# Norms ahead of the feed-forward stages in two halves of the tokens, and four PSUM banks at the merge

## What is computed

```python
# block a
mixed = sigmoid(ga) * ya + sigmoid(gb) * yb           # yb = r @ w_b
x = x + mixed @ w_out
h2 = x * rsqrt(mean(x * x) + EPS) * g_mlp              # over the features
x = x + square(relu(h2 @ w_up)) @ w_down
# block b
merged = sigmoid(gate_a) * ya + sigmoid(gate_b) * yb
x = layer_norm(DN_ALPHA * x + merged @ w_out + b_out, ln1_g, ln1_b)
x = layer_norm(DN_ALPHA * x + conv_ffn(x), ln2_g, ln2_b)
```

## Time and profile before

| | |
|---|---|
| median of three runs | 3595.11 us |
| the profiled execution | 3596.14 us |
| its span, first to last instruction | 3594.4 us |
| mean granted clock of TensorE | 0.985 |
| busy: PE, DVE, ACT, POOL | 3444.3, 1591.8, 1432.2, 1445.8 us |

### The profile page before, as it was taken

The page is one execution under the profiler, slowest core; times in us unless marked ns, Lnnn a source line. Parts: engine busy times, 40 slices in busy tenths (PEclk is TensorE's granted clock), DMA queues, the critical chain, the costliest instruction groups (busy, mean ns, idle before and its releaser), DMA issues.

```text
span 3594.4 us, 45460 instructions
## 1 busy us (share of the span) xinstructions
PE 3444.3 (96%) x16338; PEld 2792.4 (78%) x16338; DVE 1591.8 (44%) x2423; ACT 1432.2 (40%) x2114; POOL 1445.8 (40%) x1100
## 2 busy tenths in 40 slices
PE   7999999999999999999999999999999999999997
PEld 6788778887688778887768876787777688767785
DVE  5724232226623332227861444434478514344435
ACT  4735233224734332224462444333344534353333
POOL 3334444444334444444323342444343233434442
PEclk9999999999999999999999999999999999999999
DMA  3121222222112222222212121222212121222221
GB/s 142 59 83 71 94 93 95 93 95 94 69 72 91 91 88 94 94 105 73 83 36 83 68 88 71 94 93 93 82 72 71 54 75 61 95 69 94 93 93 59
DMA packets 43812, 298.49 MB, mean 83 GB/s; under 512 B 4816, under 2 KB 5456, under 8 KB 8592
## 3 DMA queue, kind: packets, MB, share of 16 engines
q1 hardware_dynamic: 41696, 291.52, 22.7%
q10 hardware_dynamic: 1968, 4.94, 0.4%
HBM read 294.34 MB, written 2.10 MB: 82 GB/s over the span
## 4 chain that ended last, share of the span: by engine, by line
issue 54%; POOL 32%; PE 11%; DVE 1%; ACT 1%; POOLq 1%; DVEq 0%; ACTq 0%
POOL w_lo L310 32%; PE ps L432 4%; PE ps L434 3%; PE ps L433 3%; PE ps L516 0%; POOLq L305 0%; DVE arena L1640 0%; ACT arena L1115 0%; POOLq L309 0%; DVE x L1675 0%; DVE arena L1663 0%; DVE tmp L1470 0%; ACT y_hi L1134 0%; DVE x L1912 0%; ACT x L1433 0%
## 5 line engine op out<-in xcount | busy, mean ns | idle before, releaser
L310 POOL TENSOR_TENSOR w_lo<-w_raw,w_hi 128x512 fp32r<-128x512 f32 x1096 | 1445.6, 1351 | 2106.1 <-ACT w_hi L936 2106.1
L432 PE MATMUL ps<-x_hi,w_hi 128*128 128x512 f32 x2752 | 1098.9, 399 | 23.0 <-DVE x_lo L1455 18.4
L433 PE MATMUL ps<-x_lo,w_hi 128*128 128x512 f32 x2752 | 1076.8, 391 | 0.0
L434 PE MATMUL ps<-x_hi,w_lo 128*128 128x512 f32 x2752 | 1076.7, 391 | 0.0
L936 ACT ACTIVATE w_hi<-w_raw 128x1024 fp32r<-128x1024 f32 x548 | 547.5, 1048 | 503.9 <-PE ps L434 503.9
L432 PEld LDWEIGHTS ps<-x_hi,w_hi 128*128 128x128 f32 x2752 | 519.9, 189 | 172.2 <-issue 38.1
L434 PEld LDWEIGHTS ps<-x_hi,w_lo 128*128 128x128 f32 x2752 | 519.7, 189 | 111.3
L433 PEld LDWEIGHTS ps<-x_lo,w_hi 128*128 128x128 f32 x2752 | 520.4, 189 | 106.0 <-issue 2.4
L432 PE MATMUL ps<-y_hi,w_hi 128*128 128x512 f32 x1248 | 490.9, 393 | 20.4 <-DVE x L1675 13.0
L433 PE MATMUL ps<-y_lo,w_hi 128*128 128x512 f32 x1248 | 487.1, 390 | 0.0
L434 PE MATMUL ps<-y_hi,w_lo 128*128 128x512 f32 x1248 | 486.7, 390 | 0.0
(11 more groups left out here) (184 smaller groups left out, 3139.0 us busy)
## 6 DMA issues: line engine op xcount, KB each, us to landing
w_raw<-stream SPq DMA_DIRECT2D x274, 1024.0 KB, 4.8
x<-x_t SPq DMA_DIRECT2D x4, 512.0 KB, 5.7
rotary<-rot ACTq DMA_DIRECT2D x4, 512.0 KB, 3.6
y_t<-x SPq DMA_DIRECT2D x8, 256.0 KB, 2.1
ct<-consts ACTq DMA_DIRECT2D x2, 770.0 KB, 4.7
arena<-pos ACTq DMA_DIRECT2D x2, 256.0 KB, 3.4
vec<-vectors ACTq DMA_DIRECT2D x4, 116.0 KB, 2.0
ct<-consts ACTq DMA_DIRECT2D x1, 128.0 KB, 4.1
```

Of the source, the lines that this page charges most:

```text
L310: ins = nc.gpsimd.tensor_tensor(WL[:, s, c:c + S], RAW[:, s, c:c + S], WH[:, s, c:c + S].bitcast(F32), ALU.subtract)
L432: pe.matmul(ps, wh, xh, start=(k == 0), stop=False)
L433: pe.matmul(ps, wh, xl, start=False, stop=False)
L434: return pe.matmul(ps, wl, xh, start=False, stop=last)
```

## The change

Three things are changed. First, in `mixer_gemms` of TensorE the ring of banks is 4 long from the last gates on. Second, wo panels 2 and 3 are worked by `gemm_halves`: all four tiles for tokens 0 to 255, then all four for tokens 256 to 511; the first two up panels are worked the same way (`first_up`). So a panel's slot is released only in the second half. Third, the norm ahead of the feed-forward stage (n2 in a, ln1 in b; twice each) is made for each half by itself: its small products stand in TensorE's order at the places given as `beside`, and the steps of DVE and ACT, each on 256 columns, are written out in an order that mixes both halves with the additions of wo and the casts of the panels. `keep_clock` is gone from these four norms. ACT's `hi` can now be issued in two parts (`hi_first`, `hi_part`). The norm ln2 of block b and the ones at the start of the layers stay. The four negated sinks are computed behind the norm of a layer instead of ahead of it.

The diff, cut to its core (the first part is TensorE's, then ACT's, then DVE's; blank lines are left out):

```diff
+            def gemm_halves(n, xh, xl, name, beside):
...
+                banks = [next_bank(name(j)) for j in range(4)]
+                for h in range(2):
+                    for j in range(4):
+                        s = (n + j // 2) % 2
+                        if h == 0 and j % 2 == 0:
+                            pe.wait_ge(lo_ready, n + j // 2 + 3)
+                        T.after(("read",) + name(j) + (0,) if h else bank_reader[banks[j]], own=False)
+                        for k in range(KD):
+                            c = (k * 2 + j % 2) * P
+                            mm = split_products(PS[:, banks[j], HS[h]], k, k == KD - 1, WH[:, s, c:c + P], WL[:, s, c:c + P],
+                                                xh[:, k, HS[h]], xl[:, k, HS[h]])
+                        T.done(mm, *name(j), h)
+                        if h:
+                            bank_reader[banks[j]] = ("read",) + name(j) + (1,)
+                            if j % 2:
+                                marks[("panel", n + j // 2)] = marks[name(j) + (1,)]
+                        if (h, j) in beside:
+                            beside[h, j]()
...
+            def mixer_gemms(l, w, t, gates, beside):
+                ring[0] = 4
                 for _ in gates:
...
-                for p in range(4):
+                for p in range(2):
                     (gemm if p else gemm_first)(w["wo"] + p, KD, 2, XH, XL, lambda k: (t, l, "merged_lo", k),
                          lambda m: (t, l, "wo", 2 * p + m))
-
-            def ffn(l, t, ff, groups, kt, base_t, base_d, base_h, h_ready):
+                gemm_halves(w["wo"] + 2, XH, XL, lambda j: (t, l, "wo", 4 + j), beside)
...
+            def ffn(l, t, ff, groups, kt, base_t, base_d, base_h, h_ready, beside):
...
-                for b in range(4):
-                    T.after(bank_reader[b], own=False)
+                def first_up():
+                    if l or t == "b":
+                        pe.wait_ge(up_read, base_t)
+                    for h in range(2):
+                        for p in range(2):
+                            if h == 0:
+                                pe.wait_ge(lo_ready, ff + p + 3)
+                                T.after(*bank_reader[2 * p:2 * p + 2], own=False)
+                            s = (ff + p) % 2
+                            for k in range(KD):
+                                if p == 0:
+                                    T.after(h_ready(k, h), own=False)
+                                for m in range(2):
+                                    c = (k * 2 + m) * P
+                                    mm = split_products(PS[:, 2 * p + m, HS[h]], k, k == KD - 1, WH[:, s, c:c + P],
+                                                        WL[:, s, c:c + P], XH[:, k, HS[h]], XL[:, k, HS[h]])
+                                    if h and k == KD - 1:
+                                        mm.then_inc(up_full, 1)
+                                if (h, p, k) in beside:
+                                    beside[h, p, k]()
...
-                        if isinstance(g, int) and g == 0 and p == 0:
...
+                mixer_gemms(l, w, t, gates, {(1, 0): lambda: deviation(0), (1, 1): lambda: spread_half(0)})
+                ffn(l, t, w["ff"], FF1_GROUPS, 4, *bases(t, l), lambda k, h: (t, l, "h2_lo", k, h),
+                    {(0, 0, 2): lambda: deviation(1), (0, 0, 6): lambda: spread_half(1)})
...
+                def mean(h):
...
+                    T.after((t, l, "ln1_sum", KD - 1, h), bank_reader[bank], own=False)
+                    T.done(pe.matmul(PS[:, bank, 0:HN], CT[:, 128:256], TMP[:, 2, HS[h]], start=True, stop=True),
+                           t, l, "ln1_mean", h)
...
+                def mean_square(h):
+                    bank = 5 + 2 * h
+                    T.after(bank_reader[bank], own=False)
+                    for k in range(KD):
+                        T.after((t, l, "ln1_sq", k, h), own=False)
+                        mm = pe.matmul(PS[:, bank, 0:HN], CT[:, 128:256], AR[:, 20 + k, HS[h]], start=(k == 0), stop=(k == KD - 1))
+                    T.done(mm, t, l, "ln1_ms", h)
...
+                mixer_gemms(l, w, t, gates, {(1, 0): lambda: mean(0), (1, 2): lambda: mean_square(0)})
+                ffn(l, t, w["ff"], FF2_GROUPS, 2, *bases(t, l), lambda k, h: (t, l, "ln1_lo", k, h),
+                    {(0, 0, 6): lambda: mean(1), (0, 1, 7): lambda: mean_square(1)})
...
+            def hi_first(c):
+                act.wait_ge(raw_full[c % 2], 16 * (c // 2 + 1))
+                who, n = marks.get(("panel", c - 2), ("pe", 1))
+                act.wait_ge(sems[who], n)
+                hi_part(c % 2, 0)
...
+                def square(k, *h):
+                    c = HS[h[0]] if h else slice(0, S)
+                    free = max(k - 2, 1)
+                    A.after(("read", t, l, "wo", k, *h), (t, l, "n2_acc", free, *(h if free >= 4 else ())) if k >= 2 else None)
+                    A.done(act.activation(TMP[:, k % 2, c], X[:, k, c], ACT.Square), t, l, "n2_sq", k, *h)
...
+                hi(w["wo"] + 2)
+                square(0)
+                square(1)
+                hi(w["wo"] + 3)
+                square(2)
+                square(3)
+                warm_root()
+                for k in range(4, KD):
+                    square(k, 0)
+                half_root(0)
+                square(4, 1)
+                hi(w["ff"])
+                square(5, 1)
+                for k in range(4):
+                    half_hi(0, k)
+                square(6, 1)
+                half_hi(0, 4)
+                square(7, 1)
+                hi_first(w["ff"] + 1)
+                half_hi(0, 5)
+                half_hi(0, 6)
+                hi_part((w["ff"] + 1) % 2, 1)
+                half_hi(0, 7)
+                half_root(1)
+                for k in range(KD):
+                    half_hi(1, k)
...
+                def half_x(h, k):
+                    g = VB["ln1_g"] + k
+                    A.after((t, l, "ln1_scaled", k, h))
+                    A.done(act.activation(X[:, k, HS[h]], X[:, k, HS[h]], ACT.Identity, scale=VEC[:, l % 2, g:g + 1],
+                                          bias=VEC[:, l % 2, g + 8:g + 9]), t, l, "ln1_x", k, h)
+                    split_hi(XH[:, k, HS[h]], X[:, k, HS[h]], [(t, l, "wo", 7, h)], (t, l, "ln1_hi", k, h))
...
+                hi(w["wo"] + 2)
+                hi(w["wo"] + 3)
+                warm_root()
+                half_squares(0)
+                hi(w["ff"])
+                half_root(0)
+                half_x(0, 0)
+                half_x(0, 1)
+                hi_first(w["ff"] + 1)
+                half_x(0, 2)
+                half_x(0, 3)
+                hi_part((w["ff"] + 1) % 2, 1)
+                for k in range(4, KD):
+                    half_x(0, k)
+                half_squares(1)
+                half_root(1)
+                for k in range(KD):
+                    half_x(1, k)
+                for k in range(KD):
+                    A.after((t, l, "ln1_lo", k, 0), (t, l, "ln1_lo", k, 1))
+                    A.done(act.activation(X[:, k, :], X[:, k, :], ACT.Copy, scale=DN_ALPHA), t, l, "x2_scaled", k)
+                ffn(l, t, w["ff"], FF2_GROUPS, 2, *bases(t, l))
...
+                def half_scaled(h, k):
+                    g = VA["g_mlp"] + k
+                    V.after(*[(t, l, "h2_hi", k - 2, h), (t, l, "h2_lo", k - 2, h)] if k >= 2 else [(t, l, "n2_spread", h)],
+                            own=False)
+                    V.done(dve.scalar_tensor_tensor(TMP[:, k % 2, HS[h]], X[:, k, HS[h]], VEC[:, l % 2, g:g + 1],
+                                                    PS[:, 7 - 2 * h, 0:HN], ALU.mult, ALU.mult), t, l, "n2_scaled", k, h)
...
+                add_out(t, l, 0)
+                add_out(t, l, 1)
+                add_out(t, l, 2)
+                square_sum(1)
+                add_out(t, l, 3)
+                square_sum(2)
+                add_out(t, l, 4, 0)
+                square_sum(3)
+                for k in range(5, KD):
+                    add_out(t, l, k, 0)
+                    square_sum(k - 1, 0)
+                square_sum(7, 0)
+                add_out(t, l, 4, 1)
+                half_inverse(0)
+                add_out(t, l, 5, 1)
+                square_sum(4, 1)
+                half_tiles(0, 0, 1, 2, 3, 4)
+                add_out(t, l, 6, 1)
+                square_sum(5, 1)
+                half_tiles(0, 5)
+                add_out(t, l, 7, 1)
+                square_sum(6, 1)
+                square_sum(7, 1)
+                half_tiles(0, 6, 7)
+                half_lo(0, 7)
+                half_inverse(1)
+                half_tiles(1, 0, 1, 2, 3, 4, 5, 6, 7)
+                half_lo(1, 7)
...
+                def centred(h):
+                    V.after((t, l, "ln1_mean", h))
...
+                        V.done(dve.scalar_tensor_tensor(X[:, k, HS[h]], PS[:, 4 + 2 * h, 0:HN], -1.0 / D, X[:, k, HS[h]],
```

(69 more changed lines are left out.)

183 lines of the change are left out of this document (94 added, 89 removed).

## The result

The changed kernel takes 3621.99 us (median of four, 3621.47 to 3624.73), the kernel before 3596.12 beside it: a ratio of 1.0074, 95% interval 1.0056 to 1.0091. Slower by 25.9 us, where 3619.5 was forecast. The profiled execution took 3621.47 us (span 3619.7).

What follows compares the result with a forecast made beforehand. TensorE, busy 96% of the span, was taken as the bound. Stages a at +4.3 us and b at +7.9, each twice and with the merge's -2.2 included, gave +24.4 on 3595.1: 3619.5 us, range 3596 to 3634.

Steps and rivals of the forecast that it cites:

- Bound and windows: TensorE, first wo product to end of second up panel: 82.6 us in a (+6.5), 101.6 in b (+10.1).
- Panels: Slots released late, so w_lo is late: 1.1 us before wo panel 3, 3.0 behind a's window; b's copies delay it further.
- The lock: A DVE operation with two SBUF inputs waits until the running POOL operation (1.26 us) ends; halving doubles the waits.
- The second serial chain in b: Second half's sums, root, reciprocal and first x_lo in b's norm can't be hidden: TensorE idle for 4.4 us.
- Merge: Four banks remove the bank waits at the first wb and wo products: 2.2 us less in each of four stages.
- The moved vec wait: Moved sinks and vec wait at the layers' first norm: a few small operations under TensorE's work, nothing.
- rival (4): Granted clock drops after new TensorE stalls of 2 to 5 us: +10 to +15, 3632 us; chance 0.12.
- nothing is made up: All loss falls in stretches where TensorE is the bound afterwards, so none of it is regained.
- (1): Rival: no lock to speak of between DVE and POOL, 3600 us; chance 0.12.
- (2): Rival: the norm really hides, only panel waits stay: -37, 3558 us; chance 0.10.
- (3): Rival: the halves come out even and only the four banks at the merge count: -8.8, 3586 us; chance 0.04.
- (5): Rival: half products on TensorE cost just half, 4 x 2.6 us less, 3609 us; chance 0.04.

Runs made afterwards that it cites:

- the light POOL: Kernel before and changed kernel, each with POOL's four operations on 64 columns instead of 512 from the third panel on: 3583.39 us and 3572.48 us.
- turned banks: The changed kernel with the ring of banks turned so that wo tiles 4 to 7 lie in banks 0 to 3 in every stage: 3630.46 us.

## Why the prediction was right, and where it wasn't

- **The total.** 3619.5 against 3622.0 is closer than the working earned. Forecast +24.4; the clock behind the windows added 9.4, all the rest took off 5.3, block a's windows 2.9 and the merges 0.6, and block b's windows added 0.3: +25.3 in the traces.
- **Bound and windows.** Right. In b the walk gave the end of the first half of up panel 0 at 67.1 us (measured 67.7 and 65.7), the start of its second half 13.8 behind that (13.9), the end of this half at 89.6 (90.8 and 88.8), the end of the window at 101.6 (102.8 and 100.8). In a 62.4 (60.7 and 60.4), then 17.3 us of products and a wait of 3.0 (3.2): 82.6 against 81.4 and 81.0.
- **Panels.** Right: wo panel 3 begins at 29.1 us in a where 29.7 was walked and 27.5 is the time with the light POOL; at the panel behind the window TensorE waits 3.2 us in a and 6.1 in b. With the light POOL nothing of this is left in a and 2.7 us in b, where the copies still stand ahead of the cast. That the copies make the wait in b longer was right; moved whole they gain nothing, and made in halves, mostly where ACT is idle, they gave 3.4 us in b's windows.
- **The lock.** Right, and shown in three durations and in the ends of single operations. POOL costs the second window of a 10.1 us, 81.0 against 70.9: 1.6 before wo panel 3, 5.1 more in the first half of up panel 0 (the lock, and w_lo of its own panel), 3.4 at the hand-over.
- **The second serial chain in b.** Right: 3.62 us of sums in TensorE's own order and 4.48 idle. What the prediction didn't draw from it: in b halving the norm gives nothing at all back.
- **Merge.** -8.8 forecast, -9.4 by the traces, -10.7 by its own kernel (-6.5 to -14 by the interval).
- **The moved vec wait.** "Nothing" was wrong: some 2 us at the very start. The trace of before had the row for it: DVE waits 8.57 us for the vec table ahead of its first addition (above), and I didn't ask for it.
- **The clock.** This is the step that was wrong, a term put at nothing. The mechanism was a rival with 12 in 100 and should have been a term of the sum: the waits were worked out as new idle time ahead of products that nothing paces, which is just the condition that rival (4) names, and the earlier trace rows had the price. I charged 0 and it measured 9.4; its range of 10 to 15 was nearly right. With it, and with a's windows as measured, the sum comes to 31, well inside the range still.
- **Everything else, "nothing is made up".** Of the -5.3, 1.4 is there by the first merge, with the earlier start in it, and 1.3 lies in a stretch of block b that the change doesn't touch (last section). The other 2.6 lie outside the windows and the merges too and were not followed.
- **Small walks inside.** In a, "up also waits for add 7; that lies in the same loss" is right (3.6 us earlier, nothing gained). The walk of b has no such wait; in layer 0 it is there and costs 1.7 us.
- **Rivals.** (1) falls by the durations beside POOL and by windows of 81.4 and 102.8 us where it had 77.2 and 97.2, (2) by 102.8 against 78.8, (3) by the windows. (5) falls by a stretch of the changed kernel, three half panels on end at a clock of 1.00: 144 products of 256 columns in 17.28 us, 0.120 us each, where half of a 512-column product would be 0.113.

```profile
476.94:494.22 17.28, 17.28 (x146) 17.23 (x144) 8.70 (x19) 7.70 (x15) 2.18 (x2) 1.00 0.12 51
```

## What to carry to other kernels

Working a panel of weights in halves of the tokens holds its slot until the second half, so the time to prepare the next panel is covered by half as much work: price that hand-over first. A norm in halves hides only where the second half's chain has work of the other half beside it, and each halved step of DVE can wait anew for a running POOL operation. Where the preparation is short the halves can gain: with the light POOL, 3.7 and 4.9 us a window in block a. When a new wait stands ahead of products that nothing paces, add the loss of clock behind it to the sum; where something else sets the pace, leave it out. Of this change, the two small edits, four banks at the merge and the later vec wait, make a kernel of 3582.3 us, 0.9967 of the kernel before, and the halves are what to leave.

## What the hardware showed beside this

The stretch from 1806 to 2010 us, in block b's first layer and outside the change, takes a different time in kernels that run the same instructions in it: here the kernel before, the changed one, and the one with turned banks (whose tiles may lie in other banks).

```profile
1798.37:2003.42 205.05, 193.96 (x1119) 158.15 (x1118) 83.62 (x133) 95.89 (x169) 61.95 (x48) 0.98 0.16 57
```

```profile
1806.06:2009.85 203.79, 192.51 (x1119) 157.42 (x1118) 83.83 (x133) 95.84 (x169) 61.91 (x48) 0.98 0.16 57
```

```profile
1808.99:2017.65 208.66, 197.28 (x1119) 161.03 (x1118) 83.86 (x133) 95.85 (x169) 61.89 (x48) 0.96 0.16 56
```

Up to 4.9 us apart, with the same busy time on every engine but TensorE; its PE differs by 4.8, and the granted clock is 0.96 instead of 0.98. The banks aren't needed for it: the merge alone and the merge with the vec wait run the same instructions on the same banks here, and take 206.75 and 203.66 us. Which parts of the stretch run at the lower level changes from kernel to kernel: from 130 to 140 us into it the granted clock is 1.00 in the kernel before, 0.83 in the changed one and 0.66 in the one with turned banks. This is as large as most effects sought here, so single terms were read from the windows that an edit touches, and differences of 2 to 5 us between medians are left open where no window shows them. What sets which way it goes was not tried.
